# Splitting the low halves of the weights into more operations outside the dense part of the feed-forward layers

## The chip, the cores and the metric

The kernel runs on one core of a Trainium2 chip. The metric is the device time of one execution in microseconds (us); a version's time is the median of its runs. The engines are TensorE (PE in the profile, PEld for its weight loads), VectorE (DVE), ScalarE (ACT), GpSimd (POOL) and SyncE (SP), which here only issues loads and the final store.

## What is computed

The reference is a network on 256 tokens of width 1024, in float32. Two blocks (16 meta tokens ahead, so 272 columns) have a mixer of retention, a gated linear recurrence and differential attention, and a feed-forward layer with a short convolution:

```python
h = h + mixer(rms_norm(h, norm_mix_g[li]), w_in[li], w_branch[li], w_out[li], ...)
h = h + conv_ffn(rms_norm(h, norm_ffn_g[li]), w_ffn_in[li], conv_w, conv_b, w_ffn_out[li], valid)
...
gate, val = jnp.split(c, 2, axis=-1)
return (jax.nn.silu(gate) * val) @ w_ffn_out
```

After them come a mixer with latent attention and a recurrence (`ev_...` weights) and one with a state-space layer (`od_...`). Behind each of these stand a cross-attention (`xa_...`) and a feed-forward layer without convolution (`ffn_w13`, `ffn_w2`), on 256 columns. The hidden width of all four feed-forward layers is 2816, which is 22 tiles of 128.

## The kernel before, in words

Activations lie transposed: features on partitions (tiles of 128), tokens along the free axis (NT = 272 or NS = 256 columns). A projection multiplies weights in pieces. A piece is one column of 128 output features with up to eight k-tiles of 128 input features, so 128 x 1024 float32 at most. Each weight is used as a high part (rounded to fp32r) and a low part (what is left), and so is each activation. The function `three` (L2226) computes one k-tile by three matmuls: high weight with high activation, high weight with low activation, low weight with high activation. A full piece is thus 24 matmuls.

The order of all pieces is fixed by `walk`, which each engine runs through with its own functions. `PIECES` lists them; there are 669. For piece g:
- SyncE (`sp_project`, L311) waits until the last low part of piece g-4 is made (L316) and loads the weights into one of four `raw` buffers (L317).
- ScalarE (`a_split`, L324) waits for the load and for the matmuls of piece g-4, and writes the high parts of the whole piece into one of four `wh` buffers in one operation (L331). It does this three pieces ahead of TensorE.
- GpSimd (`g_split`, L333) waits for that, and subtracts: `wl = raw - wh`, four k-tiles (128x512) per operation (L341). So a piece of eight k-tiles takes two operations, one of six takes one 128x512 and one 128x256, one of four takes one. Each operation signals `("lo", g, k)` for its k-tiles. Beside a few copies and fills GpSimd does nothing else.
- TensorE (`pe_project`, L391) waits for the low parts at k = 0, 3 and 4 (L403) and for the activations, and runs the matmuls (all recorded at L275). Between k-tiles it takes steps of background work (attention, recurrences), where `walk` gives it some.
- VectorE and ScalarE take the results out of PSUM and do everything else: norms, gates, softmax, splits of activations. L636 (low part of the next operand), L644 (sum of squares), L753 and L759 belong to the norms; L1066 and L1067 to the gated recurrence; L1772, L1783 and L1808 to the GLU; L1602 to the gates; L588 and L502 read PSUM.

`glu` (L1857) runs the first matrix of a feed-forward layer in 11 groups of 256 columns, each with a gate and a value projection (four pieces a group, 44 in all). `res` (L3397) runs a projection whose result is added to the residual; with 22 k-tiles it has chunks of 8, 8 and 6 for each of 8 output columns. `cross` (L3407) runs a cross-attention; its output projection has four k-tiles, and `pe_x_early` (L2214) runs the first three k-tiles of its first three pieces ahead.

Of the kernel before, what the change touches and what calls it, by code (L numbers as in the profile page):

```python
# [8 lines left out]
F32 = mybir.dt.float32  # L9
# [7 lines left out]
P = 128  # L17
NT = 272
NM = 16
PW = 25300  # L20
NS = 256
MLT, ADD, SUB, MAX, MIN = ALU.mult, ALU.add, ALU.subtract, ALU.max, ALU.min
# [46 lines left out]
class Points:  # L69
# [21 lines left out]
    def sig(self, name, *points):  # L91
        return self.up(name, 1, points)
# [7 lines left out]
    def at(self, *point):  # L100
        return self.value[point] if self.counted else (None, 1)
# [58 lines left out]
def drain(bg):  # L160
    for _ in bg:
        pass
# [36 lines left out]
def program(nc, A, out_ap, ctx):  # L199
    def sb(name, shape, dt=F32):  # L200
        return ctx.enter_context(nc.sbuf_tensor(name, shape, dt))

    points = Points(nc, ctx)
    sig, at, last, landed = points.sig, points.at, points.last, points.landed
# [8 lines left out]
    h = sb("h", [P, 8, NT])  # L213
# [89 lines left out]
    PIECES = []  # L303

    def plan_project(E, p):
        for k0, kn in p.chunks:
            for a in range(0, p.cn, P):
                PIECES.append((p.W[:, k0:k0 + kn, p.c0 + a:p.c0 + a + P], kn))
        return iter(())

    def sp_project(E, p):  # L311
# [8 lines left out]
    def piece_views(g):  # L320
        n = PIECES[g][1] * P
        return [x[g % m][:, 0:n].rearrange("p (k c) -> p k c", c=P) for x, m in ((raw, NRAW), (WH, NHL), (WL, NHL))]
# [10 lines left out]
    def g_split(E, g):  # L333
        if g >= len(PIECES):
            return
        src, hi, lo = piece_views(g)
        E.e.wait_ge(*at("hi", g))
        kn = PIECES[g][1]
        for k in range(0, kn, 4):
            ks = slice(k, min(k + 4, kn))  # L340
            E.e.tensor_tensor(lo[:, ks, :], src[:, ks, :], hi[:, ks, :].bitcast(F32), SUB).then_inc(  # L341
                *sig("weight_lo", *[("lo", g, i) for i in range(k, min(k + 4, kn))]))

    def a_prime(E):
        for g in range(NHL - 1):
# [45 lines left out]
    def pe_project(E, p):  # L391
        e, rr = E.e, E.many(p)
        for k0, kn in p.chunks:
            for mi in range(len(p.js)):
                g, r = E.piece(), rr[mi] if rr else E.banks(1)[0]
                o = banks[place(p, p.js[mi], r)][:, 0:p.n]
                if k0 == 0 and p.aux.get("wide"):
                    wide_free(E, mi, r)
                elif k0 == 0 and r >= 3:
                    e.wait_ge(*at("out", r - 3))  # L400
                for k in range(3 if p.js[mi] < p.aux.get("early", 0) else 0, kn):
                    kk = k0 + k
                    if k % 4 == 0 or k == 3:  # L403
                        e.wait_ge(*at("lo", g, k))
                    key = p.aux.get("made", E.ep)
                    if (key, kk) not in E.ready:
                        E.ready.add((key, kk))
                        e.wait_ge(*at("xl", key, kk))
                    xh, xl = operand(E, p, kk)
                    m = three(E, g, o, xh, xl, k, kk == 0, kk == p.KT - 1)  # L410
                    if k == kn - 1:
                        m.then_inc(*sig("piece_mm", ("mm", g)))
                    elif k % 2:
                        yield
                if k0 + kn == p.KT:
                    E.settle()
                    if p.kind in PE_EVAC:
                        PE_EVAC[p.kind](E, p, p.js[mi], r, g)
                yield
# [1437 lines left out]
    def glu(E, name, W, n, conv, halfway=None):  # L1857
        Wv = W.rearrange("(k p) c -> p k c", p=P)
        E.rest, E.lo, E.conv = [], [], conv is not None
        c = "c" if conv else ""  # L1860
        for a in range(0, HID, 256):
            scaled = a < 512 or not conv
            if a == 1536 and halfway is not None:
                E.do(halfway)
            x, aux = ("u1" if conv else "u2", dict(made=f"u{E.nid}")) if scaled else ("x", {})
            E.run(E.part["project"](E, Proj(name + "g", Wv, 8, a, 256, a // P, n, x, c + "gate", conv=conv, scaled=scaled, **aux)))
            E.run(E.part["project"](E, Proj(name + "v", Wv, 8, HID + a, 256, a // P, n, x, c + "val", conv=conv, scaled=scaled, **aux)))
        E.do("glu_end", name)
        E.ep += 1
# [344 lines left out]
    def pe_x_early(E, i):  # L2214
        e = E.e
        for k in range(3):
            e.wait_ge(*at("xl", f"xo{i}", k))
            E.ready.add((f"xo{i}", k))
        for n in range(3):
            g, r = E.g + n, E.r + n  # L2220
            e.wait_ge(*at("lo", g, 2))
            e.wait_ge(*at("out", r - 3))
            for k in range(3):
                three(E, g, banks[r % 3][:, 0:NS], XH[:, k, 0:NS], XL[:, k, 0:NS], k, k == 0, False)
# [1164 lines left out]
    hs_ = h[:, :, NM:NT]  # L3389
# [7 lines left out]
    def res(E, name, W, KT, x, n, add, src, nn, following, which, **aux):  # L3397

        E.nid += 1
        E.do("table")  # L3400
        linear(E, name, W, KT, 0, 1024, x, n, "res", add=add, src=src, nn=nn, next=(following,), which=which, **aux)
# [21 lines left out]
    def ffn(E, i):  # L3423
        norm(E, hs_, NS, f"fn{i}")
        glu(E, f"g{i}", A["ffn_w13"][i], NS, None)
        res(E, f"fo{i}", A["ffn_w2"][i], 22, "hid", NS, hs_, None if i else hs_, NS, "odn", "u2")

    def walk(E):
        E.do("begin")
# [3 lines left out]
        for li in range(2):  # L3433
            def w_in(name, kind, bg=None, rate=0.0, **aux):
                linear(E, f"{name}{li}", A["w_in"][li], 8, AT_IN[name], dict(W_IN)[name], "x", NT, kind, bg, rate, **aux)

            bg = E.bg("scalars") if li == 0 else None
            linear(E, f"hf{li}", A["w_in"][li], 8, AT_IN["hf"], 1024, "u1", NT, "copy", bg, 0.25, dst=HK, scaled=True,
                   made=f"u{E.nid}")
            if bg is not None:  # L3440
                drain(bg)
            bg = E.bg("hgrn_prep", li)
            w_in("hq", "copy", bg, 0.22, dst=HQ)
            w_in("hi", "tm", bg, 0.22, dst=HV, toks=TOK, tiles=8)
            drain(bg)
            bg = E.bg("hgrn", li)
            w_in("dq", "rope", bg, 0.78, dst=DQ, rope=("p2", "c2", "s2", 0.125))
            w_in("dk", "rope", bg, 0.78, dst=DK, rope=("p2", "c2", "s2", 1.0))
            w_in("dv", "tm", bg, 0.78, dst=DV, toks=TOK, tiles=8)
            w_in("rq", "rope", bg, 0.78, dst=RQ, rope=("p1", "c1", "s1", 1.0))  # L3450
            w_in("rk", "rope", bg, 0.78, dst=RK, rope=("p1", "c1", "s1", 1.0))
            drain(bg)
            bg = E.bg("diff", li)
            w_in("hg", "copy", bg, 0.82, dst=HGR)
            w_in("rv", "tm", bg, 0.82, dst=RV, toks=TOK, tiles=8)
            w_in("mg", "copy", bg, 0.82, dst=MG)
            drain(bg)
            if li:
                E.do("gains")
            bg = chain(E.bg("split_do", li), E.bg("gates", li), E.bg("ret", li), E.bg("rgate", li), E.bg("split_rg", li))  # L3460
            w_in("rg", "copy", bg, 0.4, dst=RG)
            E.do("split_bh", li)
            linear(E, f"br{li}2", A["w_branch"][li, 2], 8, 0, 1024, "do", NT, "branch", bg, 0.4, branch=2, base=True, li=li,
                   made=f"do{li}")
            E.do_done = E.g - 1
            linear(E, f"br{li}1", A["w_branch"][li, 1], 8, 0, 1024, "x", NT, "branch", bg, 0.4, branch=1, base=False, li=li,
                   made=f"bh{li}")
            E.bh_done = E.g - 1
            drain(bg)
            linear(E, f"br{li}0", A["w_branch"][li, 0], 8, 0, 1024, "rg", NT, "branch", branch=0, base=False, li=li,  # L3470
                   made=f"rg{li}")
            E.settle()
            res(E, f"wo{li}", A["w_out"][li], 8, "x", NT, h, h, NT, f"nf{li}", "u1", made=f"yb{li}")
            norm(E, h, NT, f"nf{li}")
            glu(E, f"f{li}", A["w_ffn_in"][li], NT, (f"cw{li}", f"cb{li}"), "second" if li else None)
            if li == 0:
                res(E, f"fl{li}", A["w_ffn_out"][li], 22, "hid", NT, h, h, NT, "nm1", "u1")
                norm(E, h, NT, "nm1")
        res(E, "fl1", A["w_ffn_out"][1], 22, "hid", NT, h, hs_, NS, "both", "x")
        E.do("queries")  # L3480
        norm(E, hs_, NS, "both")
        WI = A["ev_w_in"]
# [223 lines left out]
```

## Time and profile before

| | us |
|---|---|
| median of 3 runs | 2931.2 |
| lowest, highest | 2931.2, 2941.18 |
| profiled execution | 2948.53 |
| its span, first to last instruction | 2946.7 |

| engine | busy us | share of the span | instructions |
|---|---|---|---|
| TensorE | 2661.7 | 90% | 19244 |
| VectorE | 1615.7 | 55% | 2811 |
| ScalarE | 1343.1 | 46% | 2361 |
| GpSimd | 1803.7 | 61% | 1343 |

The profile is of one execution, the one of 2948.53 us. "The chain that ended last" goes back from the last instruction, at each step to what released it or to the instruction before it on its engine. A group's line gives the line, engine and operation, output<-inputs, the shape and the count, then the busy time and the mean of one, and behind the second bar the idle time of the engine just before. Timeline rows with "x2" or more merge consecutive operations of one kind, from the start of the first to the end of the last.

### The profile page before, as it was taken

How to read it: one execution, taken by the hardware profiler on the slowest of the kernel's cores; microseconds unless marked ns; L12 is line 12 of the kernel's file. 1: busy time of each engine (PE TensorE's matmuls, PEld its weight loads, DVE VectorE, ACT ScalarE, POOL GpSimd, SP SyncE). 2: the span in 40 equal slices, each digit the busy share in tenths (PEclk: the TensorE clock that was granted, in tenths of full speed). 3: DMA queues.
4: the chain of work that ended last, by engine and by line, in shares of the span. 5: the costliest groups of instructions: out<-in, count | busy, mean ns of one | idle time of the engine just before them, and what ended most of it. 6: DMA issues, size and time to landing. Idle time of an engine off the chain costs nothing.

```text
span 2946.7 us, 48712 instructions
## 1 busy us (share of the span) xinstructions
PE 2661.7 (90%) x19244; PEld 2469.4 (84%) x19244; DVE 1615.7 (55%) x2811; ACT 1343.1 (46%) x2361; POOL 1803.7 (61%) x1343
## 2 busy tenths in 40 slices
PE   6889999999999899999989988868779987888899
PEld 6878889898999788888989985658779986678899
DVE  5875333478547864323787375644454366565541
ACT  4424445455545244445556534531344443355443
POOL 5745546687888455456969871310349973346797
PEclk9999999999999999999999998869889998899999
DMA  6423334455655223344547651100136652223565
GB/s 189 129 75 97 102 108 129 118 155 148 175 168 147 85 81 114 102 117 127 159 125 213 180 152 49 54 26 1 43 101 184 180 153 79 69 83 112 154 187 150
DMA packets 682594, 354.88 MB, mean 120 GB/s; under 512 B 10912, under 2 KB 680704, under 8 KB 681856
## 3 DMA queue, kind: packets, MB, share of 16 engines
q1 hardware_dynamic: 680416, 343.45, 40.6%
q10 hardware_dynamic: 1952, 8.31, 0.8%
q8 instruction: 154, 2.52, 0.3%
q14 instruction: 72, 0.59, 0.1%
HBM read 350.67 MB, written 1.05 MB: 119 GB/s over the span
## 4 chain that ended last, share of the span: by engine, by line
PE 67%; DVE 19%; issue 5%; ACT 4%; POOL 3%; DMA 1%; DVEq 0%; SPq 0%; ACTq 0%
PE pb L275 66%; POOL wl L341 3%; DVE bx L644 2%; ACT pool L298 1%; DVE pool L1067 1%; DVE xl L753 1%; DVE u2l L636 1%; DVE bx L3098 1%; ACT wh L331 1%; ACT rs L298 1%; DVE bx L759 1%; DMA raw<-in_w_in 1%; DVE pool L1066 1%; DVE rgr L636 1%; DVE pool L3137 1%
## 5 line engine op out<-in xcount | busy, mean ns | idle before, releaser
L341 POOL TENSOR_TENSOR wl<-raw,wh 128x512 fp32r<-128x512 f32 (+1 forms) x1322 | 1787.5, 1381 | 964.0 <-ACT wh L331 962.7
L275 PE MATMUL pb<-xh,wh 128*128 128x272 f32 (+1 forms) x3104 | 958.8, 309 | 34.4 <-DVE xl L777 9.8
L275 PE MATMUL pb<-xh,wl 128*128 128x272 f32 (+1 forms) x3104 | 907.8, 292 | 0.0
L275 PE MATMUL pb<-xl,wh 128*128 128x272 f32 (+1 forms) x3104 | 906.2, 292 | 0.0
L331 ACT ACTIVATE wh<-raw 128x1024 fp32r<-128x1024 f32 (+2 forms) x669 | 688.8, 1032 | 437.9 <-PE pb L275 382.3
L275 PEld LDWEIGHTS pb<-xh,wh 128*128 128x128 f32 x3104 | 603.8, 195 | 58.3 <-issue 27.8
L275 PEld LDWEIGHTS pb<-xl,wh 128*128 128x128 f32 x3104 | 604.7, 195 | 3.8 <-issue 0.2
L275 PEld LDWEIGHTS pb<-xh,wl 128*128 128x128 f32 x3104 | 602.7, 194 | 0.0
L275 PE MATMUL pb<-pool 128*128 128x128 f32 (+13 forms) x2064 | 348.5, 319 | 76.4 <-DVE pool L1067 28.5
L275 PEld LDWEIGHTS pb<-pool 128*128 128x128 f32 (+6 forms) x2064 | 256.1, 187 | 146.3 <-DVE pool L1067 33.8
L275 PE MATMUL pb<-u2h,wh 128*128 128x256 f32 x840 | 245.9, 293 | 16.3 <-DVE u2l L636 14.7
L275 PE MATMUL pb<-u2l,wh 128*128 128x256 f32 x840 | 240.6, 286 | 0.0
L275 PE MATMUL pb<-u2h,wl 128*128 128x256 f32 x840 | 240.4, 286 | 0.0
L275 PE MATMUL pb<-hidh,wl 128*128 128x272 f32 (+1 forms) x704 | 200.7, 285 | 0.0
L275 PE MATMUL pb<-hidh,wh 128*128 128x272 f32 (+1 forms) x704 | 200.0, 284 | 0.0
L275 PE MATMUL pb<-hidl,wh 128*128 128x272 f32 (+1 forms) x704 | 199.7, 284 | 0.0
L298 ACT ACTIVATE pool<-pool 128x256 f32<-128x256 f32 (+6 forms) x173 | 120.9, 702 | 162.6 <-DVE pool L1053 77.0
L275 PE MATMUL pb<-dor,wh 128*128 128x272 f32 x512 | 156.6, 306 | 40.8 <-DVE rgr L636 28.9
L275 PEld LDWEIGHTS pb<-u2h,wh 128*128 128x128 f32 x840 | 163.5, 195 | 19.0 <-DVE u2l L636 16.1
L662 DVE TENSOR_TENSOR h<-h,pb 128x256 f32<-128x256 f32 (+1 forms) x80 | 33.7, 423 | 248.6 <-PE pb L275 248.3
L275 PEld LDWEIGHTS pb<-u2l,wh 128*128 128x128 f32 x840 | 163.4, 195 | 0.7
L275 PEld LDWEIGHTS pb<-u2h,wl 128*128 128x128 f32 x840 | 163.4, 195 | 0.0
(341 smaller groups left out, 4038.0 us busy)
## 6 DMA issues: line engine op xcount, KB each, us to landing
raw<-in_w_in SPq DMA_DIRECT2D x208, 512.0 KB, 3.7
raw<-in_ffn_w SPq DMA_DIRECT2D x120, 512.0 KB, 3.9
raw<-in_w_ffn_in SPq DMA_DIRECT2D x88, 512.0 KB, 3.8
raw<-in_w_branch SPq DMA_DIRECT2D x48, 512.0 KB, 3.9
raw<-in_od_w_in SPq DMA_DIRECT2D x41, 512.0 KB, 3.8
raw<-in_w_ffn_out SPq DMA_DIRECT2D x32, 512.0 KB, 4.0
raw<-in_ev_w_in SPq DMA_DIRECT2D x20, 512.0 KB, 4.0
raw<-in_w_out SPq DMA_DIRECT2D x16, 512.0 KB, 3.9
```

The lines of the kernel that those rows point to most:

```text
L275: return e.matmul(out, lhsT=l, rhs=r, start=a, stop=z, skip_group_check=True)
L298: return E.e.activation(o, i, f, bias=bias, scale=scale)
L331: E.e.activation(hi, src, ACT.Copy).then_inc(*sig("weight_hi", ("hi", g)))
L341: E.e.tensor_tensor(lo[:, ks, :], src[:, ks, :], hi[:, ks, :].bitcast(F32), SUB).then_inc(*sig("weight_lo", *[("lo", g, i) for i in range( ...
L636: e.scalar_tensor_tensor(out=lo[:, k, 0:n], in0=src[:, k, :], scalar=gain(gname, k), in1=hi[:, k, 0:n].bitcast(F32), op0=MLT, op1=SUB).the ...
L644: e.tensor_tensor(BX[:, 0, 0:n], BX[:, 0, 0:n], square_slot(k)[:, 0:n], ADD).then_inc(*sig("norm_acc", ("acc", E.nid, k)))
L662: E.e.tensor_tensor(x, x, banks[place(p, j, r)][:, 0:p.n], ADD).then_inc(*sig("residual", ("out", r), ("h", E.nid, j)))
L753: e.tensor_tensor(XL[:, i, 0:n], BX[:, i % 4, 0:n], XH[:, i, 0:n].bitcast(F32), SUB).then_inc(*sig("x_lo_v", ("xl", E.ep, i)))
L759: e.scalar_tensor_tensor(out=BX[:, i % 4, 0:n], in0=src[:, i, :], scalar=vc(gname, i), in1=rs[:, 1, 0:n], op0=MLT, op1=MLT).then_inc(*sig( ...
L1066: e.tensor_tensor(halves(Wk, t0, s, 0), halves(Wk, t0, s, 0), halves(k_, t0, s, 0), MLT)
L1067: m = e.tensor_tensor(halves(Wk, t0, s, 1), halves(Wk, t0, s, 1), halves(q_, t0, s, 1), MLT)
L3098: m = e.scalar_tensor_tensor(out=c[:, q:NS], in0=o[:, 0:NS - q], scalar=vc("scw", 4 * j + 3 - q), in1=c[:, q:NS], op0=MLT, op1=ADD)
```

## The change

`PIECES` gets a third entry: how many k-tiles one GpSimd operation covers. It is 4 for projections with the flag `dense`, else 2. The flag is set for the column groups of `glu` from column 512 on and for the down-projections of all four feed-forward layers. `g_split` makes its operations of that size: in all other projections a piece of eight k-tiles takes four operations of 128x256, one of four k-tiles two. TensorE waits at each multiple of that number and at k = 3. `pe_x_early` waits for k = 1 too. The order of the pieces, the buffers, and what ScalarE and VectorE run stay as they were.

```diff
--- before.py
+++ after.py
@@ -305,7 +305,7 @@
     def plan_project(E, p):
         for k0, kn in p.chunks:
             for a in range(0, p.cn, P):
-                PIECES.append((p.W[:, k0:k0 + kn, p.c0 + a:p.c0 + a + P], kn))
+                PIECES.append((p.W[:, k0:k0 + kn, p.c0 + a:p.c0 + a + P], kn, 4 if p.aux.get("dense") else 2))
         return iter(())
 
     def sp_project(E, p):
@@ -335,11 +335,12 @@
             return
         src, hi, lo = piece_views(g)
         E.e.wait_ge(*at("hi", g))
-        kn = PIECES[g][1]
-        for k in range(0, kn, 4):
-            ks = slice(k, min(k + 4, kn))
-            E.e.tensor_tensor(lo[:, ks, :], src[:, ks, :], hi[:, ks, :].bitcast(F32), SUB).then_inc(
-                *sig("weight_lo", *[("lo", g, i) for i in range(k, min(k + 4, kn))]))
+        _, kn, part = PIECES[g]
+        for k in range(0, kn, part):
+            ks = range(k, min(k + part, kn))
+            s = slice(ks[0], ks[-1] + 1)
+            E.e.tensor_tensor(lo[:, s, :], src[:, s, :], hi[:, s, :].bitcast(F32), SUB).then_inc(
+                *sig("weight_lo", *[("lo", g, i) for i in ks]))
 
     def a_prime(E):
         for g in range(NHL - 1):
@@ -400,7 +401,7 @@
                     e.wait_ge(*at("out", r - 3))
                 for k in range(3 if p.js[mi] < p.aux.get("early", 0) else 0, kn):
                     kk = k0 + k
-                    if k % 4 == 0 or k == 3:
+                    if k % PIECES[g][2] == 0 or k == 3:
                         e.wait_ge(*at("lo", g, k))
                     key = p.aux.get("made", E.ep)
                     if (key, kk) not in E.ready:
@@ -1863,6 +1864,7 @@
             if a == 1536 and halfway is not None:
                 E.do(halfway)
             x, aux = ("u1" if conv else "u2", dict(made=f"u{E.nid}")) if scaled else ("x", {})
+            aux["dense"] = a >= 512
             E.run(E.part["project"](E, Proj(name + "g", Wv, 8, a, 256, a // P, n, x, c + "gate", conv=conv, scaled=scaled, **aux)))
             E.run(E.part["project"](E, Proj(name + "v", Wv, 8, HID + a, 256, a // P, n, x, c + "val", conv=conv, scaled=scaled, **aux)))
         E.do("glu_end", name)
@@ -2218,6 +2220,7 @@
             E.ready.add((f"xo{i}", k))
         for n in range(3):
             g, r = E.g + n, E.r + n
+            e.wait_ge(*at("lo", g, 1))
             e.wait_ge(*at("lo", g, 2))
             e.wait_ge(*at("out", r - 3))
             for k in range(3):
@@ -3423,7 +3426,7 @@
     def ffn(E, i):
         norm(E, hs_, NS, f"fn{i}")
         glu(E, f"g{i}", A["ffn_w13"][i], NS, None)
-        res(E, f"fo{i}", A["ffn_w2"][i], 22, "hid", NS, hs_, None if i else hs_, NS, "odn", "u2")
+        res(E, f"fo{i}", A["ffn_w2"][i], 22, "hid", NS, hs_, None if i else hs_, NS, "odn", "u2", dense=True)
 
     def walk(E):
         E.do("begin")
@@ -3474,9 +3477,9 @@
             norm(E, h, NT, f"nf{li}")
             glu(E, f"f{li}", A["w_ffn_in"][li], NT, (f"cw{li}", f"cb{li}"), "second" if li else None)
             if li == 0:
-                res(E, f"fl{li}", A["w_ffn_out"][li], 22, "hid", NT, h, h, NT, "nm1", "u1")
+                res(E, f"fl{li}", A["w_ffn_out"][li], 22, "hid", NT, h, h, NT, "nm1", "u1", dense=True)
                 norm(E, h, NT, "nm1")
-        res(E, "fl1", A["w_ffn_out"][1], 22, "hid", NT, h, hs_, NS, "both", "x")
+        res(E, "fl1", A["w_ffn_out"][1], 22, "hid", NT, h, hs_, NS, "both", "x", dense=True)
         E.do("queries")
         norm(E, hs_, NS, "both")
         WI = A["ev_w_in"]
```

## Rows read from the trace of the kernel before

**Rows 1.** Page: busy time; chain by engine; two groups (busy, mean | idle).
```profile
PE 2661.7 (90%) x19244; PEld 2469.4 (84%) x19244; DVE 1615.7 (55%) x2811; ACT 1343.1 (46%) x2361; POOL 1803.7 (61%) x1343
...
PE 67%; DVE 19%; issue 5%; ACT 4%; POOL 3%; DMA 1%; DVEq 0%; SPq 0%; ACTq 0%
...
L341 POOL TENSOR_TENSOR wl<-raw,wh 128x512 fp32r<-128x512 f32 (+1 forms) x1322 | 1787.5, 1381 | 964.0 <-ACT wh L331 962.7
...
L331 ACT ACTIVATE wh<-raw 128x1024 fp32r<-128x1024 f32 (+2 forms) x669 | 688.8, 1032 | 437.9 <-PE pb L275 382.3
```
**Rows 2.** GpSimd's L341 by shape (busy, mean ns | idle before); durations min/median/max.
```profile
L341 POOL TENSOR_TENSOR wl<-raw,wh 128x256 fp32r<-128x256 f32 x32 | 23.7, 739 | 0.0
...
L341 POOL TENSOR_TENSOR wl<-raw,wh x1322: 723/1295/3821, 16.9 to 2933.5; 128x512 fp32r<-128x512 f32 x182, 128x256 fp32r<-128x256 f32 x7
```
**Rows 3.** VectorE: durations ns min/median/max; a group: busy, mean ns | idle.
```profile
L644 DVE TENSOR_TENSOR bx<-bx x70: 410/1494/1539, 25.0 to 2752.6; 128x256 f32<-128x256 f32 x42, 128x272 f32<-128x272 f32 x28
...
L588 DVE TENSOR_TENSOR pool<-pool,pb 128x272 f32<-128x272 f32 x48 | 20.8, 434 | 91.0 <-PE pb L275 90.9
```
**Rows 4.** Timeline (start, us): GpSimd, VectorE near 638 us; GpSimd undisturbed.
```profile
637.77 2.95 POOL L341 TENSOR_TENSOR wl<-raw,wh 128x512 fp32r<-128x512 f32 x2
...
639.23 2.94 POOL L341 TENSOR_TENSOR wl<-raw,wh 128x512 fp32r<-128x512 f32 x2
...
638.03 1.53 DVE L644 TENSOR_TENSOR bx<-bx 128x272 f32<-128x272 f32 x1
...
300.24 2.52 POOL L341 TENSOR_TENSOR wl<-raw,wh 128x512 fp32r<-128x512 f32 x2 [2.93 <-ACT wh L331]
```
**Rows 5.** Chain in order of time (start us, us, what), 633 to 648 us.
```profile
636.92 1.18 DVE rgr L636
638.11 1.46 DVE bx L644
```
**Rows 6.** Chain, 590 to 615 us; timeline of GpSimd and TensorE; TensorE by window.
```profile
590.36 21.04 POOL wl L341 x14
...
611.42 3.83 DMA raw<-in_w_out
...
590.36 50.36 POOL L341 TENSOR_TENSOR wl<-raw,wh 128x512 fp32r<-128x512 f32 x35 [3.33 <-ACT wh L331]
...
592.66 0.29 PE L275 MATMUL pb<-dor,wh 128*128 128x272 f32 x1
...
588.00:617.20 29.20, 29.13 (x233) 1.00 0.58 160
```
**Rows 7.** Windows, TensorE alone: us, busy (x), granted clock, DMA share, GB/s; sum.
```profile
100.00:590.00 490.00, 469.04 (x3357) 0.98 0.37 106
...
2390.00:2500.00 110.00, 82.55 (x539) 0.83 0.35 96
...
sum 2947.00, PE 2661.65; mean PE 166.35
```
**Rows 8.** Timeline of TensorE in a stretch without idle time.
```profile
2231.31 0.28 PE L275 MATMUL pb<-u2h,wl 128*128 128x256 f32 x1
2231.43 0.28 PE L275 MATMUL pb<-u2h,wh 128*128 128x256 f32 x1
```
**Rows 9.** Timeline, cross-attention output projection: GpSimd, then TensorE.
```profile
2175.58 5.59 POOL L341 TENSOR_TENSOR wl<-raw,wh 128x512 fp32r<-128x512 f32 x4 [1.22 <-ACT wh L331]
...
2177.00 0.36 PE L275 MATMUL pb<-xh,wh 128*128 128x256 f32 x1 [0.85 <-POOL wl L341]
```
**Rows 10.** Timeline of VectorE: the first and the last of the 191 operations.
```profile
21.20 0.98 DVE L636 SCALAR_TENSOR_TENSOR rgr<-h,vec,dor 128x272 fp32r<-128x272 f32 x1 [20.11 <-ACT dor L622]
...
2752.64 1.30 DVE L644 TENSOR_TENSOR bx<-bx 128x256 f32<-128x256 f32 x1
```
**Rows 11.** Windows, TensorE alone, around a stretch at the lower clock.
```profile
648.10:655.00 6.90, 6.19 (x25) 0.51 0.28 81
642.20:648.10 5.90, 3.35 (x25) 1.00 0.64 182
```

## The prediction

> **What bounds the kernel now.** I read the page first: engine busy times and the chain that ended last. TensorE is busy for 2661.7 of 2946.7 us and holds 67% of the chain; VectorE, busy only 55% of the span, holds 19% of it; GpSimd, where the changed operations run, is busy 61% and holds 3% [rows 1]. So the kernel is bound by TensorE, except where TensorE stands still for VectorE: the windows view leaves 285 us without TensorE work, and it is uneven, 21 us in the 490 us after 100 us but 27 us in the 110 us after 2390 us [rows 7]. The reader is to see that GpSimd matters little as an engine. The question is what it does to VectorE.
>
> That shows in the durations of one line. L644 (two operands, both in SBUF) takes 0.41 us at its shortest and 1.49 us at the median of 70. An operation of the same size that reads one operand from PSUM (L588, 48 of them) has a mean of 434 ns [rows 3]. In time order: GpSimd operations begin at 637.77 and 639.23 us without a pause, so the first of them ends at about 639.26 (the records of two in a row overlap by some 0.05). L644, issued at 638.03, ends at 639.56, that is 0.3 us after that end; and GpSimd pays too, since a pair takes 2.95 us there and 2.52 us where VectorE leaves it alone [rows 4]. So a VectorE operation that needs both inputs from SBUF waits for the end of the GpSimd operation under way, and gets its turn between two GpSimd operations, also between two of the same piece. The chain confirms that this is on the critical path: from 633 to 648 us it is L636 and L644 in turn [rows 5].
> The Trainium skill (SBUF — State Buffer, on the pair of ports shared by VectorE and GpSimd) says the same of whole instructions: the pair is an exclusive lock, "the loser fully blocks". By that rule an operation of half the length is half the wait; the trace agrees for 512-element operations (1.49 against 0.41 us), and no row of before shows a release at the end of a 256-element one.
>
> **Part 1: cost on GpSimd.** The flag "dense" is set for 9 of 11 column groups of each of four GLUs (4 x 9 x 4 = 144 pieces) and for the four down-projections (4 x 24 = 96). Of 669 pieces [rows 1] 429 are not dense: 413 with eight k-tiles go from two operations to four, 16 with four k-tiles from one to two, 842 operations more. A 512-element operation takes 1.295 us at the median, a pair 2.52 us; a 256-element one 0.739 us, mean of 32, all from the 6-tile pieces [rows 2, 4]. With the same overlap of 0.05 us four short ones take 4 x 0.739 - 3 x 0.05 = 2.81 us: +0.29 us for each piece of 8, +0.14 us for each of 4, in all 413 x 0.29 + 16 x 0.14 = 122 us more GpSimd time. Nearly all lies beside TensorE work; GpSimd waited 964 us for ScalarE [rows 1].
>
> Where it is not covered: from 590.36 us 35 operations run for 50.36 us without a pause, 2.88 us a piece, 3.17 after the change. TensorE needs 24 matmuls x 29.13/233 us = 3.00 us for one [rows 6]. GpSimd would fall back 0.17 us a piece, 2.9 us over 17 pieces. Its lead is 1.0 us (first operation done at 590.36 + 1.3 = 591.66, TensorE begins that piece at 592.66); shorter first and last parts give 0.55 us of lead back, and an existing later stall of TensorE absorbs some of the rest. I take 0.5 us of starving here, and the same in the second layer. The chain also runs from this stretch through 14 operations (7 pieces, 7 x 0.29 = 2.0 us later), the DMA at 611.42 that waits for the raw buffer, and ScalarE, whose queue holds the next operand's split behind the weight split [rows 6]; two shorter VectorE waits on it give 1 us back. So 1 us, twice. With 1 us for the 16 pieces of the odd output projection, that is 4 us. Bounds: 0 (leads suffice) and 24 us (the slower rival below).
>
> **Part 2: waits on TensorE.** TensorE's queue gets two more waits in each piece of eight (k = 2 and 6), one in each of four, and three in each x_early. Behind each the matmuls of that k-tile are queued. Before, a wait stands at k = 3 and 4: the matmul at 2231.43 us, behind the wait at k = 3, comes 0.12 us after the one before, the pace of all others (29.13/233 = 0.125 us at 272 columns) [rows 6, 8]. So 842 waits cost 0 to 3 ns each, 0 to 2.5 us; I take 1 us. In return k-tiles 0 and 1 are free 0.55 us earlier. That counts where TensorE starves: in the cross-attention output (pieces of four k-tiles) it begins a piece at 2177.00 right after GpSimd's first of four operations (2175.58 to 5.59 us later) [rows 9]. First half ready 0.55 us earlier, whole piece 0.14 us later: 0.4 us gained for each of two such stages, 0.8 us.
>
> **Part 3: shorter waits on VectorE.** For each VectorE operation on the chain I took its excess over the same line's and shape's free duration and the GpSimd operation whose end it waited for. 198 of them on the chain waited for operations of pieces that are not dense, 194 us in all; 9, with 10 us, for dense ones; those keep their wait. Of the 198, 191 with some saving were issued early enough that a half-length operation would have ended before: each saves at most 1.290 - 0.739 = 0.55 us. The first is at 21.20, the last at 2752.64 us [rows 10]. Sum: 104 us (many lose less than 0.55). A saving counts only as far as TensorE stands still at the end of it. Capping each group by the idle gap of TensorE that follows leaves 76 us; counting only operations that lie inside such a gap, 45 us. The low end below that is 0, if another engine's chain is always just behind. I take 52 us, near the 45, since savings made while TensorE works can be eaten by work queued before the gap. What is late next is ScalarE's part of the same norms and TensorE's own queue.
>
> **Part 4: transfers and clock.** The raw buffer is freed by the last GpSimd operation of a piece, so loads are issued up to 0.3 us later; a load lands 3.8 us after issue and waits for its turn otherwise, so nothing beyond the 2 us above. TensorE's clock was granted 0.51 from 648.1 to 655.0 us (25 matmuls in 6.9 us, where 25 x 0.125 = 3.1 us would do at 1.00), after TensorE had worked only 3.35 of 5.9 us [rows 11]. Shorter gaps can save some such stretches, shifted ones can cause others: 0, with bounds of -15 and +5 us.
>
> **Sum.** -52 - 0.8 + 4 + 1 = -48 us. The profiled execution took 2948.5 us with a span of 2946.7; the median of the three timed runs is 2931.2, 0.6% less. 2948.5 - 48 = 2900.5 for an execution like the profiled one; on the median, 2931.2 - 48 = 2883 us.
>
> **Rivals.**
> A, larger gain (0.20): savings before a gap carry over whole, and a few half-clock stretches vanish: 76 + 10 - 3 = 83 us, 2848 us. For it: in the norms VectorE and GpSimd take turns operation by operation [rows 4, 5], so every one saves its 0.55 us. Against it: TensorE is 96% busy from 100 to 590 us, where a shorter wait has little to win.
> B, little gain (0.13): the chains behind are ScalarE's and TensorE's, a quarter of 52 us is kept and the cost is as above: -13 + 5 = -8, 2923 us. For it: VectorE has only 19% of the chain, and ScalarE's steps stand between its operations.
> C, slower (0.07): GpSimd becomes the bound of the streaming stages. If VectorE slips in before every short operation, each costs 0.2 us more (2.95 against 2.52 for a pair, by two): 2.81 + 4 x 0.2 = 3.6 us a piece against TensorE's 3.0. Over 17 pieces that is 10.2 us less some 2.5 us of lead, about 8 us in each layer, with 5 us in the odd output projection and the 2 us of the load chain twice: 25 us, 2956 us if nothing is won. It decides where a piece takes over 3.0 + 2.5/17 = 3.15 us on GpSimd. Against it: VectorE's two-input operations stay as many, so they interrupt no more often than now.
> D, the change doesn't do what it says (0.03): waits for GpSimd do not end at the end of a short operation, or the flag reaches other pieces: no change of over 5 us, 2931 us.
> The forecast has 0.57.
>
> **Chances and range.** A measurement of this kernel tells about 0.5% (15 us) from no change. Faster by more than that: forecast and A, 0.77; within: B and D, with a little of the forecast's edge, 0.16; slower: C, 0.07. The range runs from 2845 us (A: 76 us and 10 us of clock) to 2920 us (most of B's side left out with C and D, the cost bounds in): at most 2 in 10 outside.
>
> **What would show it.** GpSimd's line with 1716 operations of 128x256 and 448 of 128x512, mean of the short ones 0.74 to 0.85 us, engine busy about 1925 us. L644's median at 0.95 us instead of 1.49, L588 as before. VectorE's busy time down from 1616 us by some 150, its share of the chain below 16%. TensorE's busy time unchanged, its idle time from 285 to about 235 us, most of it gone in the norms (633 to 680) and after 2390 us. In the stretch from 590 us GpSimd near 3.2 us a piece with TensorE still at 3.0. Wrong if L644 stays at 1.49 us (D), if TensorE waits for L341 by more than 10 us in total (C), or if VectorE's waits shrink and TensorE's idle time does not (B).

## The result

The changed kernel takes 2862.2 us (median of 4 runs, 2857.6 to 2865.5), the kernel before 2934.9 us (4 runs, 2931.2 to 2941.2). The ratio is 0.9749, 95% interval 0.9722 to 0.9776: 73 us faster, where 48 were forecast. Line numbers from L308 on have moved by one to three: L341 is L342 now, L644 is L645, L636 is L637, L588 is L589.

The page of the changed kernel, profiled in an execution of 2865.45 us; busy times, the chain, the low-part line:

```profile
span 2863.6 us, 49608 instructions
...
PE 2632.5 (92%) x19244; PEld 2437.5 (85%) x19244; DVE 1518.6 (53%) x2811; ACT 1348.5 (47%) x2361; POOL 1983.4 (69%) x2185
...
PE 69%; DVE 13%; POOL 9%; ACT 4%; issue 4%; DMA 2%; DVEq 0%; SPq 0%; ACTq 0%
...
L342 POOL TENSOR_TENSOR wl<-raw,wh 128x256 fp32r<-128x256 f32 (+1 forms) x2164 | 1967.4, 945 | 705.5 <-ACT wh L331 704.9
```

Against [rows 1], GpSimd works 180 us more, and yet VectorE works 97 us less and TensorE 29 us less, though it runs the same 19244 matmuls. VectorE's share of the chain falls from 19% to 13%, GpSimd's rises from 3% to 9%. TensorE stands still for 2863.6 - 2632.5 = 231 us, before for 285 us [rows 7].

The same lines as [rows 2, 3], first GpSimd by shape, then VectorE's L645 (minimum, median, maximum) and the one that reads PSUM:

```profile
L342 POOL TENSOR_TENSOR wl<-raw,wh 128x256 fp32r<-128x256 f32 x1716 | 1371.5, 834 | 642.9 <-ACT wh L331 642.5
L342 POOL TENSOR_TENSOR wl<-raw,wh 128x512 fp32r<-128x512 f32 x448 | 598.2, 1370 | 62.6 <-ACT wh L331 62.4
```
```profile
L645 DVE TENSOR_TENSOR bx<-bx x70: 412/956/1527, 24.2 to 2673.1; 128x256 f32<-128x256 f32 x42, 128x272 f32<-128x272 f32 x28
```
```profile
L589 DVE TENSOR_TENSOR pool<-pool,pb 128x272 f32<-128x272 f32 x48 | 20.9, 436 | 82.1 <-PE pb L275 82.1
```

The counts are the ones worked out from the code. L645's median fell from 1494 to 956 ns; the one that reads PSUM took 434 ns at the mean before and 436 now. In the timeline the wait is one short operation long (GpSimd first, then VectorE, near 623 us):

```profile
622.78 0.93 POOL L342 TENSOR_TENSOR wl<-raw,wh 128x256 fp32r<-128x256 f32 x1
```
```profile
623.04 0.97 DVE L645 TENSOR_TENSOR bx<-bx 128x272 f32<-128x272 f32 x1
```

The GpSimd operation ends at 623.71, L645 at 624.01, again 0.30 us later, as in [rows 4]. The wait itself is half as long.

Not every VectorE operation is let in at the end of the first GpSimd operation, as the prediction has it of all. Some are shut out through many GpSimd operations in a row. An operation of the recurrences, VectorE first and then GpSimd beside it, before and after the change:

```profile
88.07 8.52 DVE L941 TENSOR_TENSOR pool<-pool 128x544 f32<-128x544 f32 x1
```
```profile
88.58 7.42 POOL L341 TENSOR_TENSOR wl<-raw,wh 128x512 fp32r<-128x512 f32 x6
```
```profile
110.50 11.41 DVE L942 TENSOR_TENSOR pool<-pool 128x544 f32<-128x544 f32 x1
```
```profile
107.46 13.88 POOL L342 TENSOR_TENSOR wl<-raw,wh 128x256 fp32r<-128x256 f32 x20
```

The fastest of this kind takes 0.70 us. Each of the two ends 0.6 us after GpSimd's row of operations does, and both lie on the chain almost whole. To count them: call a VectorE operation slowed if it takes 0.15 us or more above the fastest with the same operation, shape and tiles in any trace of this case. Before, 561 are slowed, by 495 us in all, and 7 of them (21 us) outlast the ends of two or more GpSimd operations. After, 678 are slowed, by 393 us, and 16 (42 us) outlast two or more. What decides which of them is shut out, no run here tells.

Where the time went, by windows of TensorE's work: both mixers' input projections, the state-space input projection, and the first pieces of the last feed-forward layer. First before, then after, the same pieces in each pair:

```profile
22.30:525.30 503.00, 471.43 (x3389) 0.97 0.38 110
859.80:1354.80 495.00, 467.15 (x3391) 0.97 0.39 112
2381.10:2641.30 260.20, 210.21 (x1269) 0.86 0.30 84
2743.80:2776.00 32.20, 26.01 (x194) 0.89 0.57 166
```
```profile
22.70:508.80 486.10, 465.80 (x3388) 0.99 0.39 114
843.20:1319.80 476.60, 460.84 (x3390) 0.99 0.40 116
2328.40:2568.60 240.20, 207.80 (x1270) 0.87 0.33 91
2667.70:2694.20 26.50, 24.23 (x196) 1.00 0.66 187
```

These four lose 61 us of the 83 between the two profiled executions. The idle time shrinks, and the granted clock is higher in each, so the same matmuls take less busy time.

### The profile page after: what moved, and what is told of

Its sections match the earlier page's. It is cut to its first block, busy times and chain, and to the rows that moved or that the text cites. A ratio compares the mean times of both kernels' runs of the same rounds, so it can differ in the third digit from the quotient of the medians.

```text
span 2863.6 us, 49608 instructions
## 1 busy us (share of the span) xinstructions
PE 2632.5 (92%) x19244; PEld 2437.5 (85%) x19244; DVE 1518.6 (53%) x2811; ACT 1348.5 (47%) x2361; POOL 1983.4 (69%) x2185
## 4 chain that ended last, share of the span: by engine, by line
PE 69%; DVE 13%; POOL 9%; ACT 4%; issue 4%; DMA 2%; DVEq 0%; SPq 0%; ACTq 0%
PE pb L275 67%; POOL wl L342 8%; DVE bx L645 1%; DVE xl L754 1%; ACT pool L298 1%; DVE bx L3101 1%; ACT wh L331 1%; ACT rs L298 1%; DMA raw<-in_w_in 1%; DVE pool L1068 1%; DVE bx L760 1%; PE pb L543 0%; DVE pool L1067 0%; DMA raw<-in_w_ffn_in 0%; PE pb L1299 0%
## 5 line engine op out<-in xcount | busy, mean ns | idle before, releaser
L342 POOL TENSOR_TENSOR wl<-raw,wh 128x256 fp32r<-128x256 f32 (+1 forms) x2164 | 1967.4, 945 | 705.5 <-ACT wh L331 704.9
L275 PEld LDWEIGHTS pb<-xh,wh 128*128 128x128 f32 x3104 | 597.5, 193 | 69.4 <-issue 35.1
L275 PEld LDWEIGHTS pb<-xl,wh 128*128 128x128 f32 x3104 | 598.6, 193 | 3.7 <-issue 0.2
L275 PE MATMUL pb<-pool 128*128 128x128 f32 (+13 forms) x2064 | 335.0, 310 | 49.5 <-DVE pool L3276 16.7
L275 PEld LDWEIGHTS pb<-pool 128*128 128x128 f32 (+6 forms) x2064 | 244.4, 180 | 117.4 <-issue 27.6
```

The source lines that it names most:

```text
L275: return e.matmul(out, lhsT=l, rhs=r, start=a, stop=z, skip_group_check=True)
L342: E.e.tensor_tensor(lo[:, s, :], src[:, s, :], hi[:, s, :].bitcast(F32), SUB).then_inc(*sig("weight_lo", *[("lo", g, i) for i in ks]))
```

## The experiments

Each is told against the kernel before with its 95% interval. The runs of the kernel before lie around 2935 us in all of them.

**Without the exception for the dense part.** Two k-tiles per operation everywhere.

```diff
-                PIECES.append((..., kn, 4 if p.aux.get("dense") else 2))
+                PIECES.append((..., kn, 2))
```

> Two k-tiles per GpSimd operation in all pieces, the dense ones too. My theory: a short operation costs GpSimd 0.29 us more a piece of eight and VectorE may interrupt it more often, so in the dense GLU parts (72 pieces at 272 columns, now 2.83 us of GpSimd against 3.0 us of TensorE; 120 pieces at 256 columns, 2.6 against 2.73 us) GpSimd becomes the bound: some 3.3 and 2.95 us a piece, together 72 x 0.3 + 120 x 0.2 + 48 x 0.1 = 50 us slower than the changed kernel, about 2912 us; TensorE waits for the low-part line by some 50 us in total. Rival (the flag makes no difference, shorter waits of VectorE win here too): within 10 us of 2862 us or below.

Measured: 2891.8 us, ratio 0.9845 (0.9817 to 0.9874), 30 us slower than the changed kernel. The direction is as expected, the size is somewhat over half. The 60 pieces of the first feed-forward layer without convolution that are dense, in the changed kernel, then here (TensorE, its weight loads, VectorE, ScalarE and GpSimd, each busy us and count):

```profile
2164.60:2328.50 163.90, 163.90 (x1396) 163.90 (x1395) 67.47 (x110) 79.49 (x112) 153.01 (x125) 1.00 0.65 188
```
```profile
2171.50:2346.00 174.50, 169.39 (x1396) 168.10 (x1395) 89.11 (x110) 78.71 (x112) 166.70 (x231) 0.98 0.60 175
```

TensorE was never idle there; now the stage is 10.6 us longer, with 5.1 us idle. GpSimd's work is 167 us where TensorE needs 164, and its lead runs out: in the changed kernel the first operation of a piece ends 3.7 us or more before TensorE begins the piece, in all 60; here 3.5 us before at the first piece, and 0.4 us or less from the 20th to the 32nd. VectorE's busy time goes up by 22 us as well, since with GpSimd always at work some of its operations are shut out: L637 takes 17.92 us from 2295.22, beside 26 GpSimd operations in a row (fastest 0.47). In this stage TensorE's recorded waits are 2.0 us for a low part and 2.9 us for VectorE. In the whole run 33 VectorE operations (129 us) outlast two or more GpSimd operations, against 16 (42 us). Over the four dense stages the two profiles differ by some 27 us (3.0, 8.6, 10.6 and 4.4). I had counted 50, and left out that a lead of about 4 us is used up first in each stage.

**Early start or short lock?** GpSimd as changed, TensorE's waits as before.

```diff
-                    if k % PIECES[g][2] == 0 or k == 3:
-                        e.wait_ge(*at("lo", g, k))
+                    if k % 4 == 0 or k == 3:
+                        e.wait_ge(*at("lo", g, min(k | 3, kn - 1)))
```

> GpSimd's operations as in the changed kernel, but TensorE waits for the low parts of four k-tiles at a time, as before, so nothing can start earlier. My theory (the gain is VectorE's shorter wait for the shared ports): at most 10 us of the 73 us are lost, 2865 to 2872 us, and L644's line keeps its new median of about 0.95 us. Rival (the gain is that TensorE starts after half as much work): most of the gain is lost, 2910 us or more.

Measured: 2867.6 us, ratio 0.9766 (0.9750 to 0.9782), and L645:

```profile
L645 DVE TENSOR_TENSOR bx<-bx x70: 411/958/1532, 24.3 to 2680.5; 128x256 f32<-128x256 f32 x42, 128x272 f32<-128x272 f32 x28
```

So starting after half a low part is worth about 5 of the 73 us. The two intervals overlap, so it may be nothing, and by their widths it is 14 us at most. The rest needs only that GpSimd's operations are short.

**One part alone, and its complement.** Short operations in the two mixers' input projections only, and in all other pieces that are not dense.

```diff
-  ... 4 if p.aux.get("dense") else 2
+  ... 2 if p.aux.get("mixin") else 4                            # e3
+  ... 4 if p.aux.get("dense") or p.aux.get("mixin") else 2      # e4
```

> Short operations only in the 208 pieces of the two mixers' input projection (w_in). By the two traces these stages lost 16.5 and 18.3 of 83 us. If each stage's gain is its own: 2934.9 - 35 x 73/83 = 2904 us. If the gain in these stages hangs on what the stages before them do, or if TensorE (96% busy there) has little to win from it as I argued: 2920 us or more.

> The complement: short operations in the other 221 pieces that are not dense, four k-tiles per operation in w_in and in the dense part. If each stage's gain is its own, the rest: 2934.9 - 48 x 73/83 = 2893 us. If the gains overlap, this one and the mixers alone add up to more than 73 us of gain, if they need each other, to less.

Measured: 2904.0 us, ratio 0.9894 (0.9879 to 0.9908), and 2885.9 us, ratio 0.9841 (0.9822 to 0.9860). The gains are 30 and 48 us, together 78 against 73, which the intervals cannot tell apart. The gains of the two parts add up. The mixers, where TensorE was 96% busy, give 30 us; I had let them count for little.

**Length against wait.** One and three k-tiles per operation outside the dense part.

```diff
-  ... 4 if p.aux.get("dense") else 2
+  ... 4 if p.aux.get("dense") else 1      # e5
+  ... 4 if p.aux.get("dense") else 3      # e6
```

> One k-tile (128x128) per GpSimd operation outside the dense part. By the two sizes measured (1.295 and 0.739 us) one takes about 0.46 us, so L644's median should fall by as much again, to about 0.68 us, if VectorE waits for exactly one operation. A piece of eight would take GpSimd 8 x 0.42 = 3.3 us undisturbed, against 2.81, and some 4 us where VectorE interrupts; in the stages without background work (branches, w_out, 64 pieces at 3.0 us of TensorE) that is 0.6 to 1 us a piece over TensorE. Forecast: the branch stages lose 10 us or more each against the changed kernel, the mixers little; together 2880 to 2900 us. Rival (the wait is all that matters): still faster than 2862 us.

> Three k-tiles per operation outside the dense part (three operations of 128x384, 128x384 and 128x256 for a piece of eight). A 128x384 one should take 1.01 us. If VectorE's wait is one operation long, L644's median is 1.2 us, between 0.96 and 1.49, and the gain lies between: half of 73 us, 2895 to 2905 us. If instead the place of the first boundary decides (TensorE's earlier start), it is near 2870 us.

Measured: one k-tile 2921.1 us, ratio 0.9955 (0.9939 to 0.9972), slower than the 2880 to 2900 us that I had expected; three 2881.9 us, ratio 0.9815 (0.9789 to 0.9842), faster than the 2895 to 2905. VectorE's durations came out much as the length of an operation asks, both times did not. L645 and GpSimd by shape, first with one k-tile, then with three:

```profile
L645 DVE TENSOR_TENSOR bx<-bx x70: 410/680/1529, 23.7 to 2722.3; 128x256 f32<-128x256 f32 x42, 128x272 f32<-128x272 f32 x28
```
```profile
L342 POOL TENSOR_TENSOR wl<-raw,wh 128x128 fp32r<-128x128 f32 x3368 | 1630.7, 522 | 426.1 <-ACT wh L331 425.2
```
```profile
L645 DVE TENSOR_TENSOR bx<-bx x70: 411/1036/1532, 24.6 to 2689.5; 128x256 f32<-128x256 f32 x42, 128x272 f32<-128x272 f32 x28
```
```profile
L342 POOL TENSOR_TENSOR wl<-raw,wh 128x384 fp32r<-128x384 f32 x842 | 926.1, 1119 | 738.1 <-ACT wh L331 736.9
```

| k-tiles per operation | L644/L645 median ns | VectorE busy us | GpSimd busy us | TensorE idle us | time us |
|---|---|---|---|---|---|
| 4 (before) | 1494 | 1616 | 1804 | 285 | 2935 |
| 3 | 1036 | 1556 | 1897 | 251 | 2882 |
| 2 (the change) | 956 | 1519 | 1983 | 231 | 2862 |
| 1 | 680 | 1514 | 2266 | 238 | 2921 |

The median for one k-tile is the 0.68 us that was worked out beforehand. Three gave 1.04 us, not 1.2: a piece of eight has two long operations and one short, and a VectorE operation meets either. Of the 70, 16 lie at 0.95 to 1.04 us and 28 at 1.22 to 1.26 us.

Below two k-tiles VectorE gains nothing more in all. It is not stopped more often (681 slowed operations against 678), and those that wait for one GpSimd operation at most lose less (248 us against 351). But 38 now outlast two or more of them, with 133 us against 42, the longest 13.12 us (L942, at 959.54, on the chain). And the cost on GpSimd takes over. From the middle of the branches on, its operations run without a pause, and TensorE waits for them:

```profile
572.55 67.67 POOL L342 TENSOR_TENSOR wl<-raw,wh 128x128 fp32r<-128x128 f32 x133 [0.54 <-ACT wh L331]
```
```profile
PEld pb L275 <- POOL wl L342: 53.6, 194, 2.2
PE pb L275 <- POOL wl L342: 11.2, 19, 1.9
```

That is 67.67 x 8/133 = 4.07 us a piece where TensorE needs 3.0. The waits hardly show as idle time in the table: most are short and fall on weight loads, while the record of the matmul ahead (0.28 us, where the next can start 0.12 us after it, [rows 8]) still runs. They show as busy time, 2682.3 us against 2632.5, though the clock is higher (0.968 against 0.962).

This is rival C's mechanism, and the branches are one of its places: they take 6.3 and 7.9 us more than in the changed kernel. But over half of the 56 us between the two profiles lies in the mixers' input projections (14.5 and 16.3 us), which I had expected to lose little, and where four VectorE operations were shut out for 10 us or more. In the changed kernel rival C acts too, but weakly:

```profile
573.62 67.06 POOL L342 TENSOR_TENSOR wl<-raw,wh 128x256 fp32r<-128x256 f32 x84
```
```profile
PEld pb L275 <- POOL wl L342: 7.7, 22, 1.0
PE pb L275 <- POOL wl L342: 4.8, 11, 1.1
```

Here a piece takes 67.06 x 4/84 = 3.19 us on GpSimd (3.17 were forecast), and TensorE waits for it for 12.5 us in all.

**The clock alone.** Extra matmuls, read by nobody, in TensorE's gaps at the norms, on the kernel before (12 and 12) and on the changed one (4 and 8).

```diff
+                        if k == 7 and r >= 3 and p.x in ("u1", "u2") and p.aux.get("scaled"):
+                            e.wait_ge(*at("out", r - 2))
+                            for _ in range(12):
+                                mm(e, banks[(r + 1) % 3][:, 0:256], WH[g % NHL][:, 0:P], WH[g % NHL][:, 0:256], True, True)
...
+        if E.g >= 4:
+            e.wait_ge(*at("hi", E.g))
+            for _ in range(12):
+                mm(e, banks[7][:, 0:256], WH[E.g % NHL][:, 0:P], WH[E.g % NHL][:, 0:256], True, True)
         e.wait_ge(*at("acc", E.nid, 7))
```

> The kernel before, with extra matmuls whose results nobody reads, 12 ahead of the wait for the last k-tile of a fresh scaled operand and 12 ahead of the wait for the norm's sum: the gaps there are 2.2 and 2.3 us long, the fillers some 1.5 us each. VectorE's waits stay as they are. It measures the clock alone. If the clock follows what TensorE did before, the half-clock stretches behind the norms (some 45 us of TensorE's work at half speed) shrink and the time falls by 8 to 20 us, to 2915 to 2927 us. If the clock has no part in it, or falls elsewhere instead: 2930 us or more (up to 10 us lost where a filler outlasts its gap).

> The changed kernel with 4 and 8 fillers at the same places (its gaps are 0.7 and 1.8 us). About 28 us of TensorE's work behind the norms still run at half speed. If the clock theory holds: 4 to 10 us below 2862 us. If the shorter gaps were all that could be had: within 3 us of it, or slower.

Measured: on the kernel before 2929.0 us, ratio 0.9983 (0.9967 to 0.9998); on the changed one 2854.7 us, ratio 0.9728 (0.9699 to 0.9756), against 0.9749 (0.9722 to 0.9776) without the fillers. TensorE in the first:

```profile
PE 2651.6 (91%) x19424; PEld 2461.5 (84%) x19424; DVE 1618.9 (55%) x2811; ACT 1343.1 (46%) x2361; POOL 1807.7 (62%) x1343
```

It runs 180 matmuls more (180 x 0.12 = 22 us) and is busy 10 us less than before, part of that because the profiled execution of the kernel before had a low clock for its kind. The granted clock rose, from a median of 0.951 over 34 executions of the kernel before to 0.9575 over 10 of this one, and VectorE's time stayed. So filling TensorE's gaps raises the clock, and this gives about 5 us (0.6 to 10 by the interval). That is below the 8 us that I had called the least; the time that the fillers themselves take where a gap is shorter was not told apart. On the changed kernel the two intervals overlap: a gain of 7 us there is not shown.

**How much is there in all?** The kernel before, with GpSimd's operations on 8 of the 128 columns of each k-tile, so that it leaves out most of the low halves.

```diff
-            E.e.tensor_tensor(lo[:, ks, :], src[:, ks, :], hi[:, ks, :].bitcast(F32), SUB).then_inc(
+            cs = slice(0, P if g < NHL else 8)
+            E.e.tensor_tensor(lo[:, ks, cs], src[:, ks, cs], hi[:, ks, cs].bitcast(F32), SUB).then_inc(
```

> The kernel before, but GpSimd subtracts only 8 of the 128 columns of each k-tile (from the fifth piece on), so most of the low halves are not computed; all waits and signals stay. It measures what all GpSimd operations together cost by the locked ports. If VectorE's excess is the wait for GpSimd, VectorE's busy time falls from 1616 us by most of its 475 us of excess, L644's median to 0.45 to 0.6 us, and the time by the 204 us of waits on the chain as far as TensorE stands still: 110 to 170 us, to 2765 to 2825 us. Rival (half of the excess comes from something else, semaphores or DMA writes into the same memory): L644 stays over 0.8 us and the time over 2860 us.

Measured: 2738.6 us, ratio 0.9327 (0.9307 to 0.9348).

```profile
PE 2580.3 (94%) x19244; PEld 2404.2 (88%) x19244; DVE 1149.3 (42%) x2811; ACT 1341.9 (49%) x2361; POOL 403.8 (15%) x1343
...
PE 85%; DVE 8%; ACT 4%; issue 3%; DMA 1%; SPq 0%; DVEq 0%; ACTq 0%; POOL 0%
```
```profile
L645 DVE TENSOR_TENSOR bx<-bx x70: 410/421/1422, 25.3 to 2543.5; 128x256 f32<-128x256 f32 x42, 128x272 f32<-128x272 f32 x28
```

VectorE loses 466 us of busy time, which is its whole excess of 475 us but 9, and L645's median is 11 ns above its minimum. No second cause is needed for the excess. The gain, 198 us, is above the 110 to 170 that I had expected from the waits on the chain. I had again left out the clock: it is 0.976 in the profiled execution, against a median of 0.951 before, and by the slope worked out below 25 x 1.5 = 38 us of the 198 go with it; 160 us are left. So about 198 us is what the length of GpSimd's operations costs the kernel before in all, and the change wins 73 of them. Nearly all of it has to come through VectorE, since TensorE waited for GpSimd only 2.0 us before; that the buffers come free earlier, and the loads with them, is in the 198 us too and was not told apart.

**A length for each stage.** From the stages of these traces: one k-tile in the state-space input projection and the cross-attention queries, three in the branches, four in the dense part, two elsewhere; and the same with the fillers.

```diff
-  ... 4 if p.aux.get("dense") else 2
+  ... 4 if p.aux.get("dense") else 3 if p.name[:2] == "br" else 1 if p.name[:2] == "xq" or p.name in ("z", "dt", "bc", "xc") else 2
```

> Operation length by stage: one k-tile in the state-space input projection and the cross-attention queries (49 pieces with background work, where one-tile operations were shorter by 6.5 and 2 us a stage), three in the branches, four in the dense part, two elsewhere. If a stage's length can be chosen on its own: 2862 - 6.5 - 4 - 2 = about 2850 us. If the short operations only move the waiting to the next stage: 2860 us or more.

> The same with the 4 and 8 filler matmuls at the norms. If the clock gain (7 us on the changed kernel) is independent: about 2843 us, and a granted clock of 0.968 or more. If the two share it: 2848 to 2852 us.

Measured: 2848.4 us, ratio 0.9705 (0.9681 to 0.9730), as forecast; with the fillers 2846.9 us, ratio 0.9700 (0.9675 to 0.9725). The first is 0.4% below the changed kernel, with intervals that just overlap (0.9722 to 0.9730); its parts were measured in single traces: the state-space input projection took 232.6 us instead of 240.0, the branches 91.4 us in both layers instead of 94.1 and 92.5. The fillers add nothing that these runs can show: 2846.9 us lies between the two outcomes that I had put against each other.

## Why the prediction was right, and where it was not

**The mechanism held, with one limit.** The median duration of L644 (now L645) follows the length of one GpSimd operation: 1.49, 1.04, 0.96, 0.68 and 0.42 us for four, three, two, one k-tile and almost none. It was the lock and not the earlier start (e2). The exception for the dense part is worth 30 us (e1). The limit: "gets its turn between two GpSimd operations" was read from one place and put as a rule for all. Most slowed operations do, but those at 88.07 us before and at 110.50 us after waited until GpSimd paused, and short operations make this more frequent, not less.

**The sum was 48 us, the measured gain 73.** The terms in turn:
- *TensorE's idle time.* Forecast from 285 to about 235 us, measured 231. This term came out as sized, but not where it was put. I had named the norms from 633 to 680 us and the part after 2390 us. From the end of the first layer's branches to its feed-forward layer only 1 us of idle time went (8.7 to 7.6); after 2381 us it was 25 us. I had capped the savings at the gap that follows each and so gave the stretch from 100 to 590 us little; the input projections of the mixers lost 11 and 12 us of idle time. The choice of 52 us between 45 and 76 was low: it already had to make good for the 12.5 us in which TensorE now waits for low parts, where 4 us had been forecast. (In the working, 191 savings of at most 0.55 us are 105 us, so a sum of 104 us means that hardly any loses less; the text says many.)
- *The clock.* Taken as 0 with a bound of -15: this is the term that was mis-sized. Between the two profiled executions TensorE's busy time fell by 29 us for the same matmuls. That pair overstates it, since the profiled execution of the kernel before had a granted clock of 0.946, the lowest of its 34 executions on record with a clock. Over these the time goes down by 1.5 us for each 0.001 of clock (standard error 0.3, correlation -0.66); the medians are 0.951 before and 0.963 after, which makes 12 x 1.5 = 18 us. 54 us of idle time and 18 us of clock are 72 of the 73 us. That fit is an estimate: the 54 us are from a pair of executions that lie 83 us apart, and the 18 us from runs of one kernel. No experiment measured this share by itself; the fillers show that the direction is causal.
- *GpSimd's cost.* Forecast +122 us, measured +180. A short operation undisturbed costs what the 32 rows of before said (0.739 us; a piece in the branches 3.19 us against 3.17). What was missed is how often VectorE stops it: the mean of the 1716 is 834 ns. VectorE's slowed operations went from 561 (495 us) to 678 (393 us): each loses less, 0.58 instead of 0.88 us, but there are more. That, and the 21 us more on those that are shut out for two or more GpSimd operations, is why VectorE's busy time fell by 97 us and not by 150. On the chain, counted as in part 3 for pieces that are not dense, they went from 198 (194 us) to 139 (79 us).
- *Where GpSimd starves TensorE.* Forecast 1.5 us a layer in the branches; the stage grew by 2.4 us in the first layer and 0.8 us in the second. The chain still leaves it through a load:

```profile
573.66 25.12 POOL wl L342 x31
...
598.80 3.53 DMA raw<-in_w_out
```

  where [rows 6] had 14 longer operations. The total of TensorE's waits for this line passed the 10 us that I had named as the sign for rival C, and the kernel was faster all the same: the sign was set too low for a gain of this size.
- *The early start.* 0.4 us for each cross-attention output was forecast; the eight pieces took 17.5 us before and 16.9 and 17.1 after. TensorE begins the piece of [rows 9] 0.88 us after GpSimd does (2129.17 against 2128.29), before 1.42. For the additional waits on TensorE e2 sets a bound: with fewer of them it is not faster. The trace of e5 has most of them, and where the low part was ready 0.25 us or more before, the matmul behind such a wait starts 125 ns after the one ahead (median of 2177), without a wait 124 ns (1136).

**The rivals.** A (larger gain, 83 us) had both its parts right in direction, the carry-over and the clock, and lies 10 us from the result, nearer than the forecast's 25: it deserved more than 0.20. B and D are out. C needs one k-tile per operation to show itself (e5), in the branches as put, and with more in the mixers' input projections, where the prediction had not put it.

## What to carry to other kernels

Where VectorE operations with both inputs in SBUF last three times as long as their fastest, look at what GpSimd runs beside them: here the length of one GpSimd operation set what most VectorE operations paid, so splitting it paid even though GpSimd's total grew. Split only where GpSimd has time to spare against the bound engine, stage by stage, and measure the piece time there. Look also for single VectorE operations of many times their fastest, beside GpSimd operations that run without a pause: shorter operations did not help these. When a gap of TensorE shrinks, count what the granted clock gives beside the gap itself; here that was about a quarter of the gain, by an estimate.

## What the runs showed of the hardware that was not expected

- The granted clock moves with small gaps, not only with long ones: with L644's median at 0.96 instead of 1.49 us, the time that TensorE spent at the lower of its two levels (1.2 GHz) was 219 instead of 315 us in the two profiled executions. With fillers on the kernel before it was 239 us.
- A VectorE operation with its inputs in SBUF can be shut out through many GpSimd operations in a row: 17.92 us for L637 with two k-tiles everywhere (fastest 0.47), 13.12 us for L942 with one k-tile (fastest 0.70). In the same traces most are let in after one.
- With GpSimd on a sixteenth of its elements, VectorE's two-input operations run at their minimum (421 against 410 ns), while the core's DMA still moves 130 GB/s over the span: the loads take nothing from VectorE that could be seen.
- A GpSimd subtraction costs 0.15 to 0.2 us beside its elements, by an estimate: in the two streams shown under the result, neighbours of 128x256 start (13.88 - 0.74)/19 = 0.69 us apart and neighbours of 128x512 (7.42 - 1.29)/5 = 1.23, which is 0.54 us for the 256 elements between, and 0.15 beside; two at 622.08 and 622.78 give 0.16.
